# Expert blocks that add their gated results into h in place, instead of storing them for a combine at the end

## The reference

```
h = x + mix
xn = rms_norm(h, norm_ffn_w)
# each token picks one group of experts, then its two best experts in that group
gate = g_p[:, None] * top_v / sum(top_v)             # two gates per token
# assignments (token, k) are sorted by expert and padded to blocks of 128 rows of one expert
hmid = silu(xb @ w_gate[e]) * (xb @ w_up[e])         # per block
out  = (hmid @ w_down[e]) * buf_w[:, None]
h    = h + segment_sum(out, token)                   # two rows per token
y    = rms_norm(h, norm_final_w)
```

## Time and profile before

| | us |
|---|---|
| median of 3 runs (lowest, highest) | 1507.23 (1505.0, 1507.36) |
| the profiled execution: its own time | 1505.11 |
| its span, first to last instruction | 1503.4 |
| PE busy | 1416.1 (94%) |
| DVE busy | 1061.5 (71%) |
| ACT busy | 766.1 (51%) |
| POOL busy | 568.4 (38%) |
| HBM read, written | 316.5 MB, 59.6 MB |

### The profile page before, as it was taken

The page is one execution under the profiler, slowest core; times in us unless marked ns, Lnnn a source line. Parts: engine busy times, 40 slices in busy tenths (PEclk is TensorE's granted clock), DMA queues, the critical chain, the costliest instruction groups (busy, mean ns, idle before and its releaser), DMA issues. The chain is left out here.

```text
span 1503.4 us, 21686 instructions
## 1 busy us (share of the span) xinstructions
PE 1416.1 (94%) x7625; PEld 1233.0 (82%) x7625; DVE 1061.5 (71%) x1225; ACT 766.1 (51%) x891; POOL 568.4 (38%) x345
## 2 busy tenths in 40 slices
PE   6999999999999999899999659999999999999976
PEld 5999999999999998788877548888888888888852
DVE  6687722366666664545463579999999999999956
ACT  6332222333333335344433438777777777777734
POOL 2323324454444442485644014333433333333311
PEclk9999999999999999999999669999999999999997
DMA  5222333234444445876653659999999999999958
GB/s 197 65 78 86 126 95 111 80 130 143 144 141 147 138 144 167 294 219 239 209 168 130 231 201 383 402 396 390 377 381 362 389 379 383 385 388 387 369 211 343
DMA packets 115793, 361.07 MB, mean 240 GB/s; under 512 B 18772, under 2 KB 48468, under 8 KB 99348
## 3 DMA queue, kind: packets, MB, share of 16 engines
q1 hardware_dynamic: 100164, 322.37, 58.6%
q0 software_dynamic: 15568, 37.87, 7.3%
HBM read 316.52 MB, written 59.64 MB: 250 GB/s over the span
## 5 line engine op out<-in xcount | busy, mean ns | idle before, releaser
L2048 DVE TENSOR_TENSOR wgu_l<-wgu,wgu_h 128x2048 fp32r<-128x2048 f32 x128 | 290.0, 2288 | 27.4 <-ACT wgu_h L1928 26.5
L1928 ACT CAST wgu_h<-wgu 128x2048 fp32r<-128x2048 f32 x124 | 237.4, 1915 | 100.6 <-PE bank0and L64 100.5
L62 PE MATMUL bank0and<-wgu_h,xh_blk 128*128 128x512 f32 x512 | 203.7, 398 | 2.9 <-DVE xl_blk L2052 2.9
L64 PE MATMUL bank0and<-wgu_h,xl_blk 128*128 128x512 f32 x512 | 200.9, 392 | 0.0
L62 PE MATMUL bank0and<-xh,wh 128*128 128x352 f32 x576 | 197.6, 343 | 3.0 <-ACT raw L906 3.0
L63 PE MATMUL bank0and<-wgu_l,xh_blk 128*128 128x512 f32 x512 | 200.3, 391 | 0.0
L64 PE MATMUL bank0and<-xh,wl 128*128 128x352 f32 x576 | 186.7, 324 | 0.0
L63 PE MATMUL bank0and<-xl,wh 128*128 128x352 f32 x576 | 186.5, 324 | 0.0
L1671 POOL TENSOR_TENSOR wol<-wo,woh 128x1024 fp32r<-128x1024 f32 x48 | 121.4, 2536 | 123.5 <-ACT woh L996 123.5
L1835 POOL DMA_INDIRECT scratch_picked<-yb,dst x31 | 92.7, 2991 | 197.5 <-DVE yb L2042 197.5
L2057 DVE TENSOR_TENSOR wd_l<-wd,wd_h 128x1024 fp32r<-128x1024 f32 x128 | 148.2, 1219 | 1.2 <-ACT wd_h L1934 1.0
(11 more groups left out here) (496 smaller groups left out, 3234.5 us busy)
## 6 DMA issues: line engine op xcount, KB each, us to landing
wgu<-in_w_gate_up SPq DMA_DIRECT2D x128, 1024.0 KB, 7.6
wd<-in_w_down SPq DMA_DIRECT2D x128, 512.0 KB, 7.6
wo<-in_w_out SPq DMA_DIRECT2D x48, 512.0 KB, 4.9
w<-in_w_in_tiles SPq DMA_DIRECT2D x36, 512.0 KB, 3.6
yy<-scratch_picked SPq DMA_DIRECT2D x8, 1024.0 KB, 12.6
scratch_xb<-stage POOLq DMA_DIRECT2D x10, 512.0 KB, 4.0
xb<-scratch_xb SPq DMA_DIRECT2D x8, 640.0 KB, 4.4
scratch_uT<-feat SPq DMA_DIRECT2D x8, 528.0 KB, 5.0
```

The source lines that it names most:

```text
L62: nc.tensor.matmul(acc, lh, rh, start=start, stop=False)
L64: return nc.tensor.matmul(acc, ll, rh, start=False, stop=stop)
L1928: nc.scalar.copy(wgu_h[:, s], wgu[:, s]).then_inc(gu_high, 1)
L2048: nc.vector.tensor_tensor(wgu_l[:, s], wgu[:, s], wgu_h[:, s].bitcast(F32), ALU.subtract).then_inc(gu_split, 1)
```

## The change

Each block's gather is doubled: besides the rows of hn it gathers its tokens' rows of h itself into `hb` (`load_base`), DVE computes `yb = gate * product + hb` in one instruction (`add_h`, in place of the copy), and the scatter writes the sums back into h. A second expert's block must see what the first one added, so the base rows of block i are gathered after the scatter of block i-1 has landed. The gates come as a column per block, `gate_row`, made at the start by 18 more matmuls. `picked`, the loads of `yy`, and the sums on DVE and PE in the combine go; h is loaded after the last scatter, and the outputs are stored by SP.

```diff
@@ experts, POOL
-            def scatter(i):
+            def load_base(i):
+                wait(pool, base_loaded, i * 16)
+                then_own(pool, nc.gpsimd.tensor_copy(base[:], of_row[:, bass.ds(i, 1)]), row_copied, i * 2 + 1)
+                wait(pool, y_done, i)
+                then_own(pool, nc.gpsimd.tensor_copy(gate_of[:], gate_row[:, bass.ds(i, 1)]), row_copied, i * 2 + 2)
                 wait(pool, y_stored, i * 16)
-                then_own(pool, nc.gpsimd.tensor_copy(dst[:], of_row[:, 1, bass.ds(i, 1)]), dst_ready, i + 1)
+                pool.indirect_dma_start(out=hb[:], out_offset=None, in_=S["h"],
+                                        in_offset=bass.IndirectOffsetOnAxis(ap=base[:], axis=0),
+                                        bounds_check=T - 1, oob_is_err=False).then_inc(base_loaded, 16)
+            def scatter(i, rows=yb):
+                then_own(pool, nc.gpsimd.tensor_copy(dst[:], of_row[:, bass.ds(i, 1)]), dst_ready, i + 1)
                 pool.wait_ge(y_done, i + 1)
-                pool.indirect_dma_start(out=S["picked"], ... in_=yb[:], ...).then_inc(y_stored, 16)
+                pool.indirect_dma_start(out=S["h"], ... in_=rows[:], ...).then_inc(y_stored, 16)
             with pool.Fori(1, m + 1) as i:
                 gather(i + 2)
                 scatter(i - 1)
+                load_base(i)
@@ experts, PE, before the loop
+            pe.wait_ge(blk_ready, 2)
+            for a in range(N_ASG):
+                last = nc.tensor.matmul(bank[2][:, 0:MAXBLK], S["place"][0:r, a, :].bitcast(F32), in_gate[0:r, a, 0:MAXBLK], ...)
+            last.then_inc(blk_psum, 1)
@@ experts, DVE, before the loop
+            nc.vector.tensor_tensor(in_gate[:], in_block[:].bitcast(F32), flat_gate..., ALU.mult).then_inc(blk_ready, 1)
...
+            dve.wait_ge(blk_psum, 2)
+            nc.vector.tensor_tensor(gate_row[:], bank[2][:, 0:MAXBLK], other, ALU.mult).then_inc(table_ready, 1)
@@ experts, DVE, in the loop
-            def unload_y(i):
+            def add_h(i, rows=yb, banks=S["banks23"]):
+                dve.wait_ge(base_loaded, i * 16 + 16)
                 wait(dve, y_stored, i * 16)
                 dve.wait_ge(down_used, i * 4 + 4)
-                nc.vector.tensor_copy(yb[:], S["banks23"][:]).then_inc(y_done, 1)
+                nc.vector.scalar_tensor_tensor(out=rows[:], in0=banks[:], scalar=gate_of[:], in1=hb[:], op0=ALU.mult, op1=ALU.add).then_inc(y_done, 1)
@@ end of experts, SP
             sp.wait_ge(y_stored, m * 16 + 32)
+            for t in range(NT + 1):
+                sp.dma_start(S["h_final"][0:rows_of(t), t, :], S["h"][...]).then_inc(S["final_loaded"][t], 16)
@@ combine: the loads of yy, the adds on DVE, the sums on PE go; per tile remain
+                after(nc.scalar.activation(junk[0:r, t % 2, :], h[0:r, t, :], ACT.Square, accum_out=st[0:r, t, 0:1]))
+                nc.scalar.activation(st[0:r, t, 1:2], st[0:r, t, 0:1], ACT.Sqrt, ...).then_inc(rms, 1)
+                after(nc.vector.reciprocal(st[0:r, t, 2:3], st[0:r, t, 1:2]))
+                nc.vector.scalar_tensor_tensor(out=h[0:r, t, :], in0=h[0:r, t, :], scalar=st[0:r, t, 2:3], in1=w[0:r, :], ...)
```

More of the change, by code:

```diff
@@ L1822, in gather @@
                 wait(pool, xg_loaded, i * 16)
-                then_own(pool, nc.gpsimd.tensor_copy(src[:], of_row[:, 0, bass.ds(i, 1)]), src_ready, i)
+                then_own(pool, nc.gpsimd.tensor_copy(src[:], of_row[:, bass.ds(i, 1)]), src_ready, i)
                 wait(pool, xT_psum, i * 2)
@@ L1842, in _ @@
                 scatter(i - 1)
+                load_base(i)
             scatter(m)
+            load_base(m + 1)
             scatter(m + 1)
[L1845 to L1850, removed]
+            load_base(m + 2)
+            scatter(m + 2, xg)
         @block.tensor
@@ L1904, in _ @@
             nc.tensor.matmul(bank[1][0:1, 0:MAXBLK], blk_col[:], C["ident"][0:MAXBLK, 0:MAXBLK], start=True, stop=True).then_inc(blk_psum, 1)
+            pe.wait_ge(blk_ready, 2)
+            for a in range(N_ASG):
+                r = P if a < 2 * NT else TS
+                last = nc.tensor.matmul(bank[2][:, 0:MAXBLK], S["place"][0:r, a, :].bitcast(F32), in_gate[0:r, a, 0:MAXBLK], start=(a == 0), stop=(a == N_ASG - 1))
+            last.then_inc(blk_psum, 1)
             pe.wait_ge(rows_ready, 1)
@@ L2021, in _ @@
             dve.wait_ge(rows_psum, 1)
-            signed = of_row_f[:, 1, :]
+            signed, other, number = (of_row_f[:, j, :] for j in range(3))
             after(nc.vector.tensor_copy(signed, bank[0][:, 0:MAXBLK]))
[L2024 to L2030, removed]
+            after(nc.vector.tensor_scalar(other, signed, 0.0, float(4 * T), ALU.is_equal, ALU.mult))
+            after(nc.vector.scalar_tensor_tensor(out=number, in0=signed, scalar=-1.0, in1=signed, op0=ALU.mult, op1=ALU.max))
+            nc.vector.scalar_tensor_tensor(out=of_row[:], in0=number, scalar=-1.0, in1=other, op0=ALU.add, op1=ALU.add).then_inc(rows_ready, 1)
             dve.wait_ge(blk_psum, 1)
             nc.vector.tensor_copy(blk_i[:, 0:MAXBLK], bank[1][0:1, 0:MAXBLK]).then_inc(table_ready, 1)
+            flat_gate = S["gate"][:].rearrange("p t k -> p (t k)")
+            nc.vector.tensor_tensor(in_gate[:], in_block[:].bitcast(F32), flat_gate.unsqueeze(2).to_broadcast([P, N_ASG, WIDE]), ALU.mult).then_inc(blk_ready, 1)
+            dve.wait_ge(rows_ready, 1)
+            after(nc.vector.tensor_scalar(other, signed, 0.0, None, ALU.is_equal))
+            after(nc.vector.tensor_tensor(other, other, signed, ALU.add))
+            after(nc.vector.reciprocal(other, other))
+            dve.wait_ge(blk_psum, 2)
+            nc.vector.tensor_tensor(gate_row[:], bank[2][:, 0:MAXBLK], other, ALU.mult).then_inc(table_ready, 1)
             def gated(i):
@@ L2075, in block_of @@
                 if not first:
[L2076 removed]
+                    add_h(i - 1)
                 low_hid(i)
@@ L2106, in combine @@
         at = S["at"]
[L2107 to L2118, removed]
+        h, w = S["h_final"], S["w_final"]
+        junk = at("junkf", 40960, [P, 2, D])
+        st = at("st_f", 49152, [P, NT + 1, 4])
+        out_stored, rms, out_ready = sem("out_stored"), sem("rms"), sem("out_ready")
         block = ctx.enter_context(nc.Block())
@@ L2123, in _ @@
         def _(sp):
[L2124 to L2150, removed]
+            for t in range(NT + 1):
+                sp.wait_ge(out_ready, t + 1)
+                dst = A["y_sample"] if t == NT else A["y_prompt"][t * P:t * P + P, :]
+                sp.dma_start(dst, h[0:rows_of(t), t, :]).then_inc(out_stored, 16)
+            sp.wait_ge(out_stored, 16 * (NT + 1))
         @block.scalar
@@ L2158, in after @@
                 then_own(act, ins, act_own, links[0])
-            for t in ORDER:
+            for t in range(NT + 1):
                 r = rows_of(t)
[L2162 to L2170, removed]
-                    after(nc.scalar.activation(junk[0:r, :], h[t][0:r, :], ACT.Square, accum_out=st[0:r, t, 0:1]))
-                    nc.scalar.activation(st[0:r, t, 1:2], st[0:r, t, 0:1], ACT.Sqrt, bias=C["eps"][0:r, :], scale=1.0 / D).then_inc(rms, 1)
+                act.wait_ge(S["final_loaded"][t], 16 if t else 32)
+                after(nc.scalar.activation(junk[0:r, t % 2, :], h[0:r, t, :], ACT.Square, accum_out=st[0:r, t, 0:1]))
+                nc.scalar.activation(st[0:r, t, 1:2], st[0:r, t, 0:1], ACT.Sqrt, bias=C["eps"][0:r, :], scale=1.0 / D).then_inc(rms, 1)
         @block.vector
```

96 lines of the change are left out of this document (35 added, 61 removed).

## The result

The changed kernel takes 1592.55 us (median of 4 runs, 1585.66 to 1595.38), the kernel before 1506.22 us: 1.057 times as long, 95% interval 1.053 to 1.060. The profiled execution took 1595.38 us, with a span of 1593.6 us.

A forecast was written before the change was run, and what follows sets the result against it. PE was taken to set the pace, DVE and DMA right behind, until a new loop of dependences outlasts a block. 1505.1 + 81 + 9 + 7.5 - 13.6 = 1589 us; range for 8 of 10: 1535 to 1627 us.

The forecast's parts named there:

- turn of the ring: Expert blocks: time from one block's sum to the next, taken as 20.5 us against 17.72, ends 18.7 and 21.75.
- 29 turns: Expert blocks: 29 intervals between sums, each 2.8 us longer, cost 81 us (29 to 117).
- 31st interval, last: End of the expert blocks, DMA engines emptying: turn taken as 17 us, the very last 11, adding 4 and 5 us.
- start: Before the first block: 18 fp32 matmuls and a DVE product delay everything by 7.5 us, ends 3 and 10.
- end: From the last scatter's issue end to the span's end: 30.8 us instead of 44.4, 13.6 less (9 to 17).
- The ring: Expert blocks: sum, scatter, its landing, base gather, its landing, next sum; this loop sets the pace, 83% for 18.3 to 22.2 us.
- five marks: After a sum: scatter issue starts +0.87, ends +3.7; landing lets base gather start +11.2; its issue ends +13.0, lands +20.4.
- the discount: Expert blocks: the summed 21.75 us lowered to 20.5, with DMA engines at 89% instead of 99%.
- The hidden ring: Expert blocks: landings shrink to 10.8 us together instead of 14.8, turn stays at 17.72 or less; 1504 us, 6%.
- DMA as the bound: Expert blocks: turn hidden, but added rows no longer fit, 0.66 us x 29 = 19; 1523 us, 6%.
- PE's clock: Expert blocks: PE's clock falls because PE stands about 3 us a block; at 0.84, 21.1 us a block, 1606 us; 5%.
- PE's idle time: Expert blocks: PE idle some 3 us a block, its down product and next gate product waiting behind DVE's sum.

The follow-up runs named there:

- e1_cut: Changed kernel without the base gather's wait on the scatter before it, the gather reading hn in place of h; 1518.04 us, 1.008 times the kernel before.
- e5_kept: Changed kernel with the base gather reading hn in place of h, its wait on the scatter before it kept; 1591.38 us.
- e9_dose3: Changed kernel with three copies of the row numbers on POOL between the scatter's landing and the base gather's issue; 1663.75 us.
- e4_table: Kernel before with only the changed kernel's gate table added at the start, read by nothing; 1515.25 us against 1505.52.
- e7_half: Changed kernel with only half of each gate/up piece loaded in the loop, in packets of 4 KB; 1504.05 us.
- e6_none: Changed kernel with the base gather's bound in the loop set to 0, so only token 0's rows are moved; 1566.95 us.
- e3_small: Changed kernel with each 1 MB gate/up load split into two of 512 KB, packets 4 KB not 8 KB; 1565.58 us, 1.040 times before.

## Why the prediction was right

Forecast 1589 us, measured 1592.55, or 1595.38 in the profiled execution, which the terms add up to; each term beside what the trace gave:

```
                           forecast   measured
turn of the ring            20.5       20.91
29 turns                    +81        +93.1
31st interval, last         +4, +5     +0.6, +4.9
start                       +7.5       +9.6, of which 2.15 ahead of the stage
end                         -13.6      -18.1
```

That the total came so close is partly luck: the turn's term was 12 us too low, and the last sums and the end together 8 us too high. The turn of 20.5 us was itself picked by judgement between 18.7 and 21.75, of which only the upper end was worked out.

**The ring** was right step by step. Counted from the sum's end, its five marks were put at 0.87, 3.7, 11.2, 13.0 and 20.4 us; the means are 0.87, 3.7, 10.9, 12.7 and 19.6. e1_cut and e5_kept show that this ring and not the traffic or the engines costs 74 us, and e9_dose3 that a delay put on it comes out at the other side. What was mis-sized is the discount. The summed turn was 21.75, and 1.25 was taken off because the DMA engines would be less loaded; the two marks gave back only 0.3 and 0.5 us. Two things lie behind the 0.3. The scatter itself landed some 0.9 us sooner than before (6.4 us after its issue's end against 7.3: seen at 1290.25 on average, less 0.15 and less 1282.78; e4_table, with the turn of before, has 7.3 too), but the mark of +11.2 was read from a small copy, which starts 0.15 us after the landing, where the base gather's issue starts 0.83 us after it; this 0.7 us a turn was missing from the sum. And the gathers land little sooner because the load that they meet has not fallen: the DMA engines, forecast at a mean of 89% and measured at 89%, are full while the base rows land. That is the reason the prediction gave for staying near the loaded rows: SP's loads go on, both landings fall among them, and only DVE's wait gives a pause. e7_half bears it out from the other side: to shorten the landings, the weights' share had to go.

**The other cases.** The hidden ring needed landings of 10.8 us together; by the same marks, with what lies between a landing and the next start, they took 7.2 + 7.0 (14.2). DMA as the bound did come true, but only in e1_cut, once the ring was cut, and at the forecast's price of 0.66 us. PE's clock stayed: 0.99 over the stretch, though PE stood in a ninth of it.

**The last two sums** were +9 and measured +5.5: the 31st turn, with emptying queues, took 13.7 us where 17 was taken.

**The start** was right for its reason: 36 matmul instructions in 8.08 us where 7.2 was taken, DVE waiting 7.38 us. The other 2.15 us are not the change's: in_block (L2016), which ends ahead of the table, ends at 873.46 against 871.31 before, and in the profiles of the other kernels here that mark lies between 869.8 and 873.4, though the changed kernel's variants have the same code ahead of it.

**The end** gave 4.5 us more than forecast. I had charged 3.1 us for leaving the block before SP's loads; they stand inside it, and the first was issued 2.3 us after the scatter's issue had ended. And from the last norm's end to the end of the span it is 2.6 us, not 4.5.

PE's idle time was forecast at some 3 us a block and is 2.3 (54 us in 23.4 turns). Its place was wrong: the prediction named the down product and the next gate product as what would wait, and PE waits mostly for the hn rows, whose gather is queued behind the base gather. That did not set the turn: each of the 23 sums in the stretch still ended its wait with the base rows.

What stays open: which part of a landing beside the weights is waiting per packet and which per byte. Smaller packets took 0.5 us off each landing. Half the weights' bytes, in those smaller packets, took 1.5 off the scatter's and 3.0 off the base gather's, and no rows 0.8 off the base gather's; no run separates them fully. A correct kernel with the ring cut was not tried; an estimate by e1_cut puts it near 1518 us, since the added rows cost 29 x 0.68 = 20 us and the start 7.5 to 9.6, and the end gives back 18.

## What to carry to other kernels

Before turning a write-only result into a read, add and write back, draw the ring that it closes and add up its landings at the load that the queues have while those transfers land (here 93% and full, at a mean of 89%), not at the idle price and not at the mean; count also the time from a landing to the start of the next issue, 0.8 us here; if the sum is over the present turn, the excess is paid every time, however idle the engines look. Then ask what is left when the ring is cut: here the added traffic, on engines at 99%, and the new table together cost more than the shorter end saved. A delay added on such a ring tests it, but part of the first dose may fall where the engine was held anyway; a second one tells.

## What the runs showed of the hardware

- An indirect transfer of 128 rows is 144 packets, whether its rows are moved or skipped by the bound (10080 packets for 70 transfers in the changed kernel, 10507 for 73 in e6_none); without its bytes it landed 0.8 us sooner, of 6.9.
- POOL's issues stretch beside DVE's long instructions: the issue of the scatter took 2.81 us beside DVE's 128x2048 low parts and 1.01 with DVE idle (at 1566.34), the gather of the hn rows 1.06 beside 128x1024 ones. A copy of 128 numbers lasted from anywhere in a long low part to its end.
- An indirect transfer's issue on POOL starts 0.83 us after the landing that it waits for, in the changed kernel, or 0.85 to 0.93 us after a POOL copy that it needs; a copy starts 0.15 us after such a landing.
- The landings went with the load while they landed and with the packets beside them, not with the mean load of the stretch (mean load; then us from the issue's end to the landing, with the load in that time, for scatter and base gather): changed kernel 0.89; 6.4 at 0.93, 6.9 with the engines full. e3_small, smaller packets, 0.95; 5.9 at 0.91, 6.4 full. e7_half 0.79; 4.9 at 0.85, 3.9 at 0.71. In the kernel before, at 0.99, the scatter and the gather of the hn rows took 7.3 us each.
- Calls of 128x128 by 49 columns in plain fp32 show as two instructions each and follow one another at 0.45 us, at a granted clock of 0.50 (1.2 GHz) from 877.24 to 885.32 us.
